# Two Strassen pairs in the output projection, their weight sums on GpSimd, and a new order around them

## The chip, the cores and the metric

One Trainium2 chip, one core of it. Every array is float32. The metric is the time of one execution of the whole program on the device, in microseconds (us); for the kernel before it is the median of three executions. The engines are TensorE (PE), VectorE (DVE), ScalarE (ACT), GpSimd (POOL) and SyncE (SP, which only issues transfers here).

## The reference, cut to what matters

One inference step of a two-layer streaming encoder, for a prompt of 256 frames and a running stream of 64 (T = 320 columns in all), at a width of 1024:

```python
for l in range(DEPTH):                      # 2 layers
    h = rms(x, norm_mix) ; proj = h @ w_in  # 14 pieces of different mixers
    y_a = head_rms(RG-LRU(conv(lru_x))) * gelu(lru_g)      # recurrence
    y_b = head_rms(latent attention)
    y_c = head_rms(retention(rope(r_q), rope(r_k), r_v)) * silu(r_g)
    y_d = head_rms(mLSTM) * sigmoid(m_o)
    x = x + concat([y_a, y_b, y_c, y_d]) @ w_out           # the output projection: 1024 x 1024
    x = x + SwiGLU(rms(x, norm_ffn))                       # hidden width 2816
```

It also returns the new states of each mixer. The line with `w_out` is what the change touches.

## The kernel before, in words

Activations lie transposed: a tile is 128 features by 320 columns, so x is 8 tiles (`xT`), the mixers' output 8 tiles (`mixT`: 0 and 1 the recurrence's, 2 and 3 attention's, 4 and 5 retention's, 6 and 7 mLSTM's). Weights come in chunks of 1 MB through a ring of five slots: SP loads chunk g once the last use of chunk g - 5 has ended (`LAST_USE`, lines 200 to 204). The four chunks of `w_out` are o0 to o3; each holds two output units of 128 features for all 8 input tiles. They are followed by f0, f1 and so on of the feed-forward part.

Every engine's program is written out by hand, in order, and engines meet at semaphores. `need` and `wait_filled` wait, `step` signals and also waits for the instruction's own end. PSUM has eight banks; `layer_uses` lists every use of a bank in a layer, `claim` lets PE wait until the use before it in the same bank has been read (`now_read`). The first head mean, `cm0`, follows the retention scores `cs2` in bank 2, which DVE reads in `weights_c(2)`.

**Strassen pairs.** Most products of the kernel are already done in a form with seven half-size products in place of eight. Two output units and 320 columns are split into 2 x 2 blocks (pairs of input tiles, halves of 160 columns). POOL makes three sums of the weight blocks by four instructions of 128x512 (`pair_weights`, lines 638 to 664, for chunks of `w_in`; `mix_weights`, 666 to 683, for the feed-forward part), the last of which signals `mixed`. Four sums of activations are made by DVE or POOL. PE runs seven products of four matmuls of 160 columns each into three banks a, b and c, and DVE adds them up in the pattern of lines 1978 to 1988 or 2406 to 2426, after ACT has copied the first product (`p1_copied`).

**The output projection** (`project(n, ks)`, line 1287) is not in this form: unit n takes one matmul of 320 columns for each of the 8 input tiles, 64 in all. The order is by what is ready: tiles 6, 7 (mLSTM) and 2, 3 (attention) first, between retention's last steps; then the recurrence's statistics `am0`, `am1` (line 1317) when `h_sq` is there; then tiles 0, 1 and 4, 5. DVE adds each finished unit to x (line 2333), ACT squares it and applies the gain (`squares`, lines 1523 and 1525), DVE sums the squares (line 2337), and PE sums them over the features (`ms2`, line 1352) in the middle of the 16 plain matmuls of the first feed-forward unit (`first_units`, line 1356).

**Around it, on the other engines.** POOL rotates retention's queries and keys (`rotate`, lines 750 to 766), stores retention's states as `c_pair` makes them, stores the recurrence's inputs and states and signals `a_out`; in layer 0 it then reloads the latents and their weights for layer 1 (`load_latents`), and goes on to the feed-forward weight sums. DVE, after the pair `rg` (1978 to 1988) and its clamp (2250), makes the recurrence's exponents (2254), retention's weights (`weights_c`, lines 2111 and 2275, four times), the recurrence's arguments (2284 to 2290), retention's gate (2293), attention's last tile (2205), `c_pair` (2264 to 2268), and the scans (2315, 2316). ACT does the roots and exponentials between. At the end DVE makes `mix0` (2325, 2326; tiles 0 and 1) and then `mix2` (2329; tiles 4 and 5).

Of the kernel before, what the change touches and what calls it, by code (L numbers as in the profile page):

```python
# [16 lines left out]
ALU = mybir.AluOpType  # L17
# [46 lines left out]
NPAIR = len(PAIRS)  # L64
MIXES = FT - 1 + 3 * NQ
MADE = NPAIR + MIXES
P1S = NPAIR + FT - 1 + NQ
# [62 lines left out]
def layer_uses():  # L130
# [44 lines left out]
    u += [(f"o{n}", (n,)) for n in range(KT)]  # L175
# [26 lines left out]
LAST_USE.update({f"o{i}": f"o{2 * i + 1}" for i in range(4)})  # L202
# [4 lines left out]
def build(nc, I, O):  # L207
    with ExitStack() as ctx:
# [136 lines left out]
        xgm = mixT  # L345
        hp = mixT[:, :, :].rearrange("p k n -> p (k n)").rearrange("p (s k n) -> p s k n", s=4, k=4)
# [273 lines left out]
        def _(pool):  # L620
# [44 lines left out]

            def mix_weights(l, i):
# [37 lines left out]
            for l in range(DEPTH):  # L704
# [63 lines left out]
                for grp in "dc":  # L768
                    if grp == "c":
# [45 lines left out]
        def _(pe):  # L815
# [240 lines left out]
            for l in range(DEPTH):  # L1056
# [230 lines left out]
                def project(n, ks):  # L1287
# [5 lines left out]
                    for k in ks:  # L1293
                        need(pe, f"mix{k // 2}", l, 1)
                        ins = mm(bank(u, 0, T), w[:, k, (n % 2) * P:(n % 2 + 1) * P], mixT[:, k, :],  # L1295
                                 start=(k == 6), stop=(k == 5), skip_group_check=True)
                    if ks[-1] == 5:
                        fill(ins, u)
# [14 lines left out]
                project(4, (6, 7, 2, 3))  # L1313
# [4 lines left out]
                project(5, (6, 7, 2, 3))  # L1318
                for n in range(2):
                    project(n, (0, 1))  # L1320
                for n in range(2):
                    project(n, (4, 5))
                for n in range(2, 6):
                    project(n, (0, 1, 4, 5))
                for n in range(6, KT):
                    project(n, (6, 7, 2, 3, 0, 1, 4, 5))

                def product(use, l, i, p, right, opens, closes):
# [3 lines left out]
                    if p in (3, 5, 6, 7):  # L1332
                        need(pe, "mixed", l, MADE, NPAIR + i + 1)
# [156 lines left out]
        def _(act):  # L1490
# [49 lines left out]
            for l in range(DEPTH):  # L1540
# [250 lines left out]
                squares(l, 1)  # L1791
# [43 lines left out]
        def _(dve):  # L1835
# [96 lines left out]
            for l in range(DEPTH):  # L1932
# [395 lines left out]
                need(dve, "c_rstd", l, 2)  # L2328
                step(v.tensor_tensor(mixT[:, 4:6, :], ycm[:, :, :], ysm[:, :, :], ALU.mult), "mix2")

                for n in range(KT):
# [3 lines left out]
                    if n > 1:  # L2335
                        need(dve, "squared", l, 2 * KT, KT + n)
# [136 lines left out]
```

How the kernel before makes its waits and increments, by code:

```python
        def wait_filled(eng, use, l):  # L420
            k = banks[use][0]
            eng.wait_ge(filled[k], l * nfill[k] + order[use])
# [1 line left out]
        def claim(pe, use, l):  # L425
            for prev in before[use]:
                if prev is not None:
                    k = banks[prev][0]
                    pe.wait_ge(read[k], l * nfill[k] + order[prev])
                elif l > 0:
                    for k in {banks[last[b_]][0] for b_ in banks[use]}:
                        pe.wait_ge(read[k], l * nfill[k])
                else:
                    top = max(banks[use])
                    pe.wait_ge(sem("x_turned"), top + 1)
                    if 0 in banks[use]:
                        pe.wait_ge(sem("cols_ready"), 1)
# [8 lines left out]
        def need(eng, name, l, n, k=None):  # L447
            assert per.setdefault(name, n) == n, name
            eng.wait_ge(sem(name), l * n + (n if k is None else k))
# [3 lines left out]
            def step(ins, name=None, bank_read=None):  # L454
                if bank_read is not None:
                    use, l = bank_read
                    k = banks[use][0]
                    ins.then_inc(read[k], 1)
                    eng.wait_ge(read[k], l * nfill[k] + order[use])
                    return
                k = name or chain
                made[k] = made.get(k, 0) + 1
                ins.then_inc(sem(k), 1)
                eng.wait_ge(sem(k), made[k])
# [11 lines left out]
        def wait_bank_read(eng, use, l):  # L476
            k = banks[use][0]
            eng.wait_ge(read[k], l * nfill[k] + order[use])
```

## Time and profile before

| | |
|---|---|
| median of 3 executions | 906.52 us (906.29 to 907.2) |
| profiled execution | 906.72 us, of which the span is 904.9 us |
| PE busy | 894.6 us (99% of the span) |
| POOL busy | 512.4 us (57%) |
| DVE busy | 511.4 us (57%) |
| ACT busy | 226.7 us (25%) |
| granted TensorE clock | 1.0 |
| moved by DMA | 112.92 MB, a mean of 125 GB/s |

The span runs from the first to the last instruction of the profile; times in the rows below count from its start. A row of the timeline has start, duration, engine, line, operation and shape, and in brackets how long the engine stood idle before and for whom. Layer 0 takes the first half of the span, layer 1 the second; the feed-forward part is more than half of each.

### The profile page before, as it was taken

Reading aid. Unit: us, or ns where it says so; the run is one execution under the profiler, and the core shown is the slowest. Engines: PE = TensorE matmul, PEld = TensorE weight load, DVE = VectorE, ACT = ScalarE, POOL = GpSimd, SP = SyncE. Lnnn points to the kernel's source line nnn. Section 1 sums busy time; section 2 is a strip of 40 time slices with the busy share of each in tenths; the row PEclk is TensorE's granted clock in tenths of the full one; section 3 lists DMA queues with packets and bytes.
Section 4 is the critical chain, followed back from the end, with each engine's and each line's share of the span. In section 5 each row is a group of like instructions: output and inputs, shape, how many; then the busy total and the mean of one; then the engine's idle time right before and its main releaser. Section 6 shows DMA issues by size and latency. Waiting matters only on the chain.

```text
span 904.9 us, 15545 instructions
## 1 busy us (share of the span) xinstructions
PE 894.6 (99%) x5984; PEld 812.3 (90%) x5984; DVE 511.4 (57%) x1001; ACT 226.7 (25%) x497; POOL 512.4 (57%) x514
## 2 busy tenths in 40 slices
PE   8999999999999999999999999999999999999998
PEld 6897878668999999999979878776799999999998
DVE  6677857735656565522366776575465656563221
ACT  3334356632000000100133334574300000000001
POOL 6861574316966666676457345902287666666770
PEclk9999999999999999999999999999999999999999
DMA  9979331239444444433444773121855545434421
GB/s 274 233 152 106 108 93 49 53 65 256 140 138 139 139 137 137 129 128 129 125 131 144 34 152 96 48 90 14 183 140 140 141 140 140 141 129 128 147 88 36
DMA packets 159091, 112.92 MB, mean 125 GB/s; under 512 B 9829, under 2 KB 156682, under 8 KB 158890
## 3 DMA queue, kind: packets, MB, share of 16 engines
q1 hardware_dynamic: 154402, 104.44, 40.2%
q0 software_dynamic: 3984, 6.74, 7.3%
q8 instruction: 48, 0.79, 0.4%
q10 hardware_dynamic: 632, 0.75, 0.3%
q14 instruction: 25, 0.20, 0.1%
HBM read 108.33 MB, written 2.27 MB: 122 GB/s over the span
## 4 chain that ended last, share of the span: by engine, by line
PE 90%; ACT 4%; DVE 4%; DMA 1%; issue 1%; POOL 0%; SPq 0%; DVEq 0%; ACTq 0%; POOLq 0%
PE ps L1338 53%; PE ps L1295 7%; PE ps L905 7%; PE ps L871 6%; PE ps L891 2%; PE ps L1356 2%; PE ps L1093 2%; PE ps L1062 1%; PE ps L1125 1%; PE ps L1221 1%; DMA arena<-in_x_sample 1%; PE ps L1229 1%; PE ps L1005 1%; DVE work L2119 1%; DVE arena L2222 0%
## 5 line engine op out<-in xcount | busy, mean ns | idle before, releaser
L680 POOL TENSOR_TENSOR work<-ring 128x512 f32<-128x512 f32 (+1 forms) x66 | 81.9, 1240 | 155.6 <-issue 111.0
L1338 PE MATMUL ps<-mixT,ring 128*128 128x160 f32 x672 | 105.0, 299 | 0.0
L1338 PE MATMUL ps<-hT,work 128*128 128x160 f32 x672 | 98.5, 299 | 0.0
L1338 PE MATMUL ps<-hT,ring 128*128 128x160 f32 x672 | 98.1, 299 | 0.0
L1338 PEld LDWEIGHTS ps<-mixT,ring 128*128 128x128 f32 x672 | 95.8, 190 | 0.0
L1338 PEld LDWEIGHTS ps<-hT,ring 128*128 128x128 f32 x672 | 93.7, 190 | 0.3
L1338 PEld LDWEIGHTS ps<-hT,work 128*128 128x128 f32 x672 | 93.7, 190 | 0.0
L681 POOL TENSOR_TENSOR ring<-ring 128x512 f32<-128x512 f32 (+1 forms) x66 | 82.6, 1252 | 5.2
L682 POOL TENSOR_TENSOR work<-ring 128x512 f32<-128x512 f32 (+1 forms) x66 | 82.0, 1243 | 5.2
L683 POOL TENSOR_TENSOR work<-ring,work 128x512 f32<-128x512 f32 (+1 forms) x66 | 81.9, 1240 | 5.2
L1805 ACT ACTIVATE arena<-ps 128x160 f32<-128x160 f32 x42 | 12.8, 304 | 286.8 <-PE ps L1338 286.8
L871 PE MATMUL ps<-hT,ring 128*128 128x320 f32 x256 | 72.9, 436 | 0.0
L1295 PE MATMUL ps<-mixT,ring 128*128 128x320 f32 x256 | 70.9, 434 | 0.9 <-DVE mixT L2326 0.9
L2406 DVE TENSOR_TENSOR arena<-arena,ps 128x160 f32<-128x160 f32 x8 | 2.6, 321 | 118.6 <-ACT arena L1823 118.6
L1295 PEld LDWEIGHTS ps<-mixT,ring 128*128 128x128 f32 x256 | 48.3, 190 | 21.6 <-issue 1.8
L871 PEld LDWEIGHTS ps<-hT,ring 128*128 128x128 f32 x256 | 47.4, 190 | 18.9 <-issue 1.0
L1338 PE MATMUL ps<-work,ring 128*128 128x160 f32 x352 | 55.6, 299 | 0.0
L1338 PE MATMUL ps<-mixT,work 128*128 128x160 f32 x336 | 52.5, 299 | 0.0
L1338 PE MATMUL ps<-arena,work 128*128 128x160 f32 x352 | 51.7, 299 | 0.0
L1338 PEld LDWEIGHTS ps<-work,ring 128*128 128x128 f32 x352 | 50.4, 190 | 0.0
L1338 PEld LDWEIGHTS ps<-arena,work 128*128 128x128 f32 x352 | 49.1, 190 | 0.0
L1338 PE MATMUL ps<-arena,ring 128*128 128x160 f32 x330 | 48.7, 299 | 0.0
(455 smaller groups left out, 1623.9 us busy)
## 6 DMA issues: line engine op xcount, KB each, us to landing
ring<-in_w_gu SPq DMA_DIRECT2D x88, 512.0 KB, 5.2
ring<-in_w_in SPq DMA_DIRECT2D x44, 512.0 KB, 6.7
ring<-in_w_down SPq DMA_DIRECT2D x32, 512.0 KB, 4.5
ring<-in_w_out SPq DMA_DIRECT2D x16, 512.0 KB, 4.9
ring<-in_w_down SPq DMA_DIRECT2D x16, 384.0 KB, 3.6
cst<-in_consts POOLq DMA_DIRECT2D x1, 1664.0 KB, 12.8
ring<-in_w_in SPq DMA_DIRECT2D x2, 640.0 KB, 5.7
arena<-r POOLq DMA_DIRECT2D x8, 160.0 KB, 18.0
```

The costliest lines, as they stand in the source:

```text
L680: step(tt(s3, a11, a21, ALU.subtract))
L681: step(tt(a21, a21, a22, ALU.add))
L682: step(tt(s2, a21, a11, ALU.subtract))
L683: step(tt(s4, a12, s2, ALU.subtract), "mixed")
L871: ins = mm(bank(use, 0, T, m), w[:, k, c:c + m], right[:, k, 0:T], start=(k == 0), stop=(k == KT - 1))
L891: ins = mm(bank(use, at * HT, HT), left, right, start=(opens and k == 0), stop=(k == KT // 2 - 1), skip_group_check=True)
L905: ins = mm(bank(use, at * HT, HT), left(k), right(k), start=(opens and k == 0), stop=(k == KT // 2 - 1), skip_group_check=True)
L1093: ins = mm(bank("kvr", t * 168, 168), hT[:, k, t * P:(t + 1) * P], w[:, k, :], start=(k == 0), stop=(k == KT - 1))
L1295: ins = mm(bank(u, 0, T), w[:, k, (n % 2) * P:(n % 2 + 1) * P], mixT[:, k, :], start=(k == 6), stop=(k == 5), skip_group_check=True)
L1338: ins = mm(bank(use, at * HT, HT), left, right(k), start=(opens and k == 0 and at == 0), stop=(closes and k == n - 1), skip_group_check=True)
L1356: return mm(bank(use, 0, T), w[:, k, q * P:(q + 1) * P], xg[:, k, :], start=(k == 0), stop=(k == KT - 1))
L1805: step(A(p1c[:, j % 2, :], bank(f"fa{j}", 0, HT), ACT.Copy), "p1_copied")
```

## The change

Units 4 to 7 (chunks o2 and o3) become two Strassen pairs, p2 and p3; units 0 to 3 stay as they were. POOL makes their weight sums right after the fourth rotation, behind a wait for `bo1` (the last reading of the attention probabilities, whose room the sums take). PE has a new order; ACT squares the recurrence's state before retention's second root; DVE makes `mix2` before `mix0`, then four sums of `mixT`, and adds up two pairs. In layer 0 `load_latents` waits for the end of both pairs, for the sums also lie in the latents' room. The counters `MADE` and `P1S` grow by two.

```diff
@@ layer_uses @@
-    u += [(f"o{n}", (n,)) for n in range(KT)]
+    u += [(f"o{n}", (n,)) for n in range(4)]
+    u += [("p2a", (4,)), ("p2c", (5,)), ("p3a", (6,)), ("p3c", (7,)), ("p2b", (0,)), ("p3b", (1,))]
@@ LAST_USE @@
-LAST_USE.update({f"o{i}": f"o{2 * i + 1}" for i in range(4)})
+LAST_USE.update({f"o{i}": f"p{i}c" if i in OUTS else f"o{2 * i + 1}" for i in range(4)})
@@ POOL @@
+            def out_weights(l, i):
+                name = f"o{OUTS[i]}"
+                w, _ = quarters(name, l)
+                s2, s3, s4 = osum[i]
+                if i == 0:
+                    wait_filled(pool, "bo1", l)
                 wait_chunk(pool, name, l)
                 a11, a12, a21, a22 = w[:, :, 0, 0, :], w[:, :, 1, 0, :], w[:, :, 0, 1, :], w[:, :, 1, 1, :]
                 tt = nc.gpsimd.tensor_tensor
...
                         for n in range(4):
                             rotate(n)
+                        for i in range(len(OUTS)):
+                            out_weights(l, i)
...
-                    wait_filled(pool, "kv2", l)
+                    for p in OUTS:
+                        wait_filled(pool, f"p{p}c", l)
                     load_latents(l + 1)
@@ PE @@
-                project(4, (6, 7, 2, 3))
+                early, late, every = (3, 1), (2,), (3, 1, 2, 0)
+                out_product(2, 1, early, opens=True)
+                out_product(2, 2, early)
+                out_product(2, 3, early, opens=True)
                 need(pe, "h_sq", l, 1)
...
-                project(5, (6, 7, 2, 3))
-                for n in range(2):
+                for n in range(4):
+                    project(n, (4, 5))
+                for which in (1, 2, 3):
+                    out_product(2, which, late)
+                out_product(3, 1, early + late, opens=True)
+                out_product(3, 2, early + late)
+                for n in range(4):
                     project(n, (0, 1))
-                for n in range(2):
-                    project(n, (4, 5))
-                for n in range(2, 6):
-                    project(n, (0, 1, 4, 5))
-                for n in range(6, KT):
-                    project(n, (6, 7, 2, 3, 0, 1, 4, 5))
+                for which in (1, 2, 3):
+                    out_product(2, which, (0,))
+                for which in (1, 2):
+                    out_product(3, which, (0,))
+                out_product(2, 6, every, closes=True)
+                out_product(2, 5, every, opens=True)
+                out_product(2, 7, every, closes=True)
+                out_product(2, 4, every, closes=True)
+                out_product(3, 6, every, closes=True)
+                out_product(3, 5, every, opens=True)
+                out_product(3, 7, every, closes=True)
+                out_product(3, 3, every, opens=True)
+                out_product(3, 4, every, closes=True)
@@ ACT @@
-                pair_rstd(1)
                 need(act, "lru_scanned", l, 1)
                 step(A(fl(an), fl(ah), ACT.Square), "h_sq")
+                pair_rstd(1)
...
-                squares(l, 1)
+                squares(l, 1, range(4))
+                for p in OUTS:
+                    need(act, "x_new", l, 2 * KT, 2 * p)
+                    wait_filled(act, f"p{p}a", l)
+                    step(A(pair_p1, bank(f"p{p}a", 0, HT), ACT.Copy), "p1_copied")
+                    squares(l, 1, range(2 * p, 2 * p + 2))
@@ DVE @@
+                need(dve, "c_rstd", l, 2)
+                step(v.tensor_tensor(mixT[:, 4:6, :], ycm[:, :, :], ysm[:, :, :], ALU.mult), "mix2")
                 for k in range(2):
                     need(dve, "a_rstd", l, 2, k + 1)
...
-                need(dve, "c_rstd", l, 2)
-                step(v.tensor_tensor(mixT[:, 4:6, :], ycm[:, :, :], ysm[:, :, :], ALU.mult), "mix2")
-
-                for n in range(KT):
+                m_at = lambda j, t: mixT[:, j::2, t * HT:(t + 1) * HT]
+                step(v.tensor_tensor(msum[0], m_at(0, 1), m_at(0, 0), ALU.subtract), "mix_sums")
+                step(v.tensor_tensor(msum[2], m_at(1, 1), msum[0], ALU.subtract), "mix_sums")
+                step(v.tensor_tensor(msum[1], m_at(1, 1), m_at(0, 1), ALU.subtract), "mix_sums")
+                step(v.tensor_tensor(msum[3], m_at(1, 0), msum[2], ALU.subtract), "mix_sums")
...
+                def out_pair(p):
+                    a, b_, c = (f"p{p}{x}" for x in "abc")
...
+                    need(dve, "p1_copied", l, P1S, NPAIR + OUTS.index(p) + 1)
+                    step(v.tensor_tensor(pair_u2, pair_p1, bank(a, HT, HT), ALU.add))
+                    step(v.tensor_tensor(x11, x11, pair_p1, ALU.add))
+                    step(v.tensor_tensor(x11, x11, bank(a, 2 * HT, HT), ALU.add), bank_read=(a, l))
+                    wait_filled(dve, b_, l)
...
+                    step(v.tensor_tensor(x22, x22, pair_u34[:, HT:T], ALU.add))
+                    step(v.tensor_tensor(x22, x22, bank(b_, 0, HT), ALU.add), bank_read=(b_, l))
+                    step(v.tensor_tensor(mid, mid, pair_u34, ALU.add))
+                    wait_filled(dve, c, l)
+                    step(v.tensor_tensor(mid, mid, bank(c, 0, T), ALU.add), "x_new")
+                    now_read(dve, c)
+                    now_made(dve, "x_new")
+
+                for n in range(4):
                     wait_filled(dve, f"o{n}", l)
...
+                for p in OUTS:
+                    squares_so_far(2 * p)
+                    out_pair(p)
+                    squares_so_far(2 * p + 1)
```

`out_product(p, which, ks)` runs product `which` of pair p for the tile pairs ks, one matmul of 160 columns for each; products 3, 5, 6 and 7 wait for `mixed`, products 4 to 7 for all four `mix_sums`. Tile pair k is made of `mixT` tiles 2k and 2k + 1. The four weight-sum instructions of `out_weights` are those of `pair_weights`.

## Rows read from the trace of the kernel before

**Rows 1.** The page, part 1: busy time, share of the span and instructions of each engine.

```profile
PE 894.6 (99%) x5984; PEld 812.3 (90%) x5984; DVE 511.4 (57%) x1001; ACT 226.7 (25%) x497; POOL 512.4 (57%) x514
```

**Rows 2.** The timeline, PE and its weight loads, layer 0: start us, us, instruction [idle before].

```profile
149.86 0.22 PE L1005 MATMUL ps<-work,arena 128*64 128x64 f32 x1
...
157.49 0.99 PE L1005 MATMUL ps<-work 128*64 128x256 f32 x12
...
164.58 0.30 PEld L1036 LDWEIGHTS ps<-work,cst 128*128 128x128 f32 x2 [0.62 <-DVEq L469]
...
175.96 2.32 PE L1295 MATMUL ps<-mixT,ring 128*128 128x320 f32 x8
```

**Rows 3.** The chain of waits: start us, us, what. Layer 0, from the output projection on.

```profile
182.02 21.77 PE ps L1295 x80
...
206.48 1.08 PE ps L1352 x4
...
213.48 237.71 PE ps L1338 x1750
```

**Rows 4.** DVE and POOL out of SBUF at once; the last is L2214's min/median/max ns.

```profile
47.38 1.32 DVE L1986 TENSOR_SCALAR work<-work 128x640 f32<-128x640 f32 x1
...
229.68 1.27 POOL L682 TENSOR_TENSOR work<-ring 128x512 f32<-128x512 f32 x1
...
231.03 1.27 POOL L683 TENSOR_TENSOR work<-ring,work 128x512 f32<-128x512 f32 x1
...
231.17 1.32 DVE L2389 TENSOR_TENSOR arena<-arena 128x160 f32<-128x160 f32 x1
...
L2214 DVE TENSOR_SCALAR wqb<-arena,cols x4: 447/449/542, 128.7 to 579.5; 128x323 f32<-128x323 f32 x4
```

**Rows 5.** The timeline, POOL, from the key rotation's end to the feed-forward sums, layer 0.

```profile
163.16 0.61 POOL L691 DMA_DIRECT2D out_p_ret<-sst  x1 [16.82 <-DVE sst L2265]
...
198.30 0.76 POOL L698 DMA_DIRECT2D pckv<-in_cache_mla_ckv  x1 [17.00 <-DMA out_s_lru_h<-arena]
...
203.67 1.26 POOL L680 TENSOR_TENSOR work<-ring 128x512 f32<-128x512 f32 x1 [3.33 <-DMA ring<-in_w_gu]
```

**Rows 6.** The w_out loads: SyncE's issues in the timeline, and on the page their landing.

```profile
131.58 18.06 SPq L587 DMA_DIRECT2D ring<-in_w_out  x4
...
ring<-in_w_out SPq DMA_DIRECT2D x16, 512.0 KB, 4.9
```

**Rows 7.** The timeline, DVE adds that read PSUM in the down projection, POOL at work.

```profile
391.32 0.32 DVE L2406 TENSOR_TENSOR arena<-arena,ps 128x160 f32<-128x160 f32 x1 [13.19 <-ACT arena L1823]
...
393.11 0.49 DVE L2414 TENSOR_TENSOR arena<-ps,arena 128x320 f32<-128x320 f32 x1
```

**Rows 8.** The timeline, DVE, from the end of rg's pair to the recurrence's result, layer 0.

```profile
150.62 0.49 DVE L2250 TENSOR_SCALAR work<-work 128x640 f32<-128x640 f32 x1
...
152.46 0.81 DVE L2254 TENSOR_SCALAR arena<-arena,c 128x323 f32<-128x323 f32 x2 [1.34 <-ACT arena L1513]
...
153.70 0.82 DVE L2275 TENSOR_TENSOR work<-ps,cst 128x384 f32<-128x384 f32 x2
...
156.56 0.83 DVE L2285 TENSOR_TENSOR arena<-arena,wqb 128x646 f32<-128x646 f32 x1
...
157.42 0.50 DVE L2287 TENSOR_SCALAR arena<-arena 128x646 f32<-128x646 f32 x1
...
159.02 1.14 DVE L2293 SCALAR_TENSOR_TENSOR work<-work,cols 128x320 f32<-128x320 f32 x2
...
161.29 0.55 DVE L2205 SCALAR_TENSOR_TENSOR mixT<-ps,cols,arena 128x320 f32<-128x320 f32 x1 [1.13 <-ACT arena L1731]
...
176.78 1.14 DVE L2321 SCALAR_TENSOR_TENSOR arena<-arena,cols 128x323 f32<-128x323 f32 x2
```

**Rows 9.** The timeline, ACT: square and gain of one x tile behind the projection, layer 0.

```profile
204.48 0.47 ACT L1523 ACTIVATE hT<-xT 128x320 f32<-128x320 f32 x1 [3.24 <-DVE xT L2333]
...
204.98 0.56 ACT L1525 ACTIVATE work<-xT,cols 128x320 f32<-128x320 f32 x1
```

More of the change, by code:

```diff
@@ L64 @@
 NPAIR = len(PAIRS)
+OUTS = (2, 3)
 MIXES = FT - 1 + 3 * NQ
-MADE = NPAIR + MIXES
-P1S = NPAIR + FT - 1 + NQ
+MADE = NPAIR + len(OUTS) + MIXES
+P1S = NPAIR + len(OUTS) + FT - 1 + NQ
 MSLOTS = 3
@@ L345, in build @@
         xgm = mixT
+        low = MSLOTS * 3 * 512 + KT * T
+        msum = [x.rearrange("p (k n) -> p k n", n=HT) for x in
+                (work[:, low:low + 4 * HT], work[:, low + 4 * HT:low + 8 * HT], work[:, low + 8 * HT:low + 12 * HT],
+                 arena[:, 2 * 326:2 * 326 + 4 * HT])]
+        pT1 = ytm_at + 640
+        osum = [[x.rearrange("p (k n) -> p k n", n=P) for x in three] for three in
+                ((pT0[:, 0:512], pT0[:, 512:1024], wkvb[:, :]),
+                 (work[:, pT1:pT1 + 512], work[:, pT1 + 512:pT1 + 1024], pckv[:, :, :].rearrange("p a n -> p (a n)")))]
         hp = mixT[:, :, :].rearrange("p k n -> p (k n)").rearrange("p (s k n) -> p s k n", s=4, k=4)
@@ L664, in pair_weights @@
                 step(tt(s4, a12, s2, ALU.subtract), "mixed")
+            def out_weights(l, i):
[4 more added lines that the diff above has]
+                    wait_filled(pool, "bo1", l)
+                wait_chunk(pool, name, l)
+                a11, a12, a21, a22 = w[:, :, 0, 0, :], w[:, :, 1, 0, :], w[:, :, 0, 1, :], w[:, :, 1, 1, :]
+                tt = nc.gpsimd.tensor_tensor
+                step(tt(s3, a11, a21, ALU.subtract))
+                step(tt(a21, a21, a22, ALU.add))
+                step(tt(s2, a21, a11, ALU.subtract))
+                step(tt(s4, a12, s2, ALU.subtract), "mixed")
             def mix_weights(l, i):
@@ L1312, in _, with out_product @@
                 pair_mean(1, l)
-                project(4, (6, 7, 2, 3))
+                def out_product(p, which, ks, opens=False, closes=False):
+                    i = OUTS.index(p)
+                    use = f"p{p}" + {1: "a", 2: "a", 6: "a", 5: "b", 7: "b", 3: "c", 4: "c"}[which]
+                    if opens:
+                        claim(pe, use, l)
+                    wait_chunk(pe, f"o{p}", l)
+                    if which in (3, 5, 6, 7):
+                        need(pe, "mixed", l, MADE, NPAIR + i + 1)
+                    if which in (4, 5, 6, 7):
+                        need(pe, "mix_sums", l, 4)
+                    w, _ = quarters(f"o{p}", l)
+                    at = {1: 0, 2: 2, 6: 1, 5: 0, 7: 1, 3: 0, 4: 1}[which]
+                    for k in ks:
+                        need(pe, f"mix{k}", l, 1)
+                        left = {1: w[:, k, 0, 0, :], 2: w[:, k, 1, 0, :], 3: osum[i][2][:, k, :],
+                                4: w[:, k, 1, 1, :], 5: w[:, k, 0, 1, :], 6: osum[i][0][:, k, :],
+                                7: osum[i][1][:, k, :]}[which]
+                        right = {1: mixT[:, 2 * k, 0:HT], 2: mixT[:, 2 * k + 1, 0:HT], 3: mixT[:, 2 * k + 1, HT:T],
+                                 4: msum[3][:, k, :], 5: msum[0][:, k, :], 6: msum[2][:, k, :], 7: msum[1][:, k, :]}[which]
+                        ins = mm(bank(use, at * HT, HT), left, right, start=(opens and k == ks[0]), stop=(k == 0),
+                                 skip_group_check=True)
+                    if closes:
+                        fill(ins, use)
+                early, late, every = (3, 1), (2,), (3, 1, 2, 0)
+                out_product(2, 1, early, opens=True)
+                out_product(2, 2, early)
+                out_product(2, 3, early, opens=True)
                 need(pe, "h_sq", l, 1)
@@ L1332, in product @@
                     if p in (3, 5, 6, 7):
-                        need(pe, "mixed", l, MADE, NPAIR + i + 1)
+                        need(pe, "mixed", l, MADE, NPAIR + len(OUTS) + i + 1)
                     for k in range(n):
```

21 lines of the change are left out of this document (14 added, 7 removed).

## The prediction

> **What bounds the kernel.** I read the page's busy shares first: TensorE (PE) is busy 99% of the span [rows 1], so time goes only where PE loses instructions or is made to wait. The chain of waits then shows the layer's one weak stretch: it leaves PE for ScalarE (ACT) and VectorE (DVE) in the middle of the mixers, comes back to PE with the first head mean at 164.6 [rows 2], and leaves it once more for the recurrence's statistics, before the output projection's last 80 records at 182.0 [rows 3]. From there on PE runs without a gap. Layer 1 repeats the pieces of layer 0 one for one, so all steps below are counted in layer 0 and doubled.
>
> Prices of PE: a matmul call leaves two records. 80 records of 320 columns took 21.77 us, so a call costs 0.544; 1750 records of 160 columns took 237.71, so a half call costs 0.272 [rows 3]. Halving the columns halves the price exactly.
>
> **PE work.** Units 4 to 7 lose 4 x 8 = 32 calls, 17.4 us. Two Strassen pairs add 2 x 7 x 4 = 56 half calls, 15.2 us. That is -2.2 us a layer, if nothing waits.
>
> **GpSimd's (POOL) eight weight sums.** POOL waits for `bo1`, the last matmul of which ends at 150.1 [rows 2], so the sums start at about 150.15. One costs 1.27, and the next begins 1.35 after it, a gap of 0.08 [rows 4]: four take 5.4, eight 10.8, some 0.7 more where DVE stretches them. They end at 161.4 to 161.7. POOL stood idle for 16.8 us until the state's store at 163.2 [rows 5], so the stores queued behind (retention's state, the recurrence's, `a_out`) start on time by themselves. Chunk o3 can only load once `rgc` is filled: its load is issued by 149.6 and takes about 4.9 [rows 6], so it lands at 154.5, before the second four sums (155.7). Nothing waits for weights: PE first wants a sum after 176.
>
> **What the sums do to DVE is the heart of it.** Rows of the feed-forward stage show what happens when both engines work out of SBUF: a DVE sum of 160 columns out of SBUF took 1.32; it began while POOL's sum of 231.03 to 232.30 ran and ended 0.19 after it [rows 4]. An add of the same size that reads PSUM took 0.32, and one of 320 columns 0.49, with POOL at work too [rows 7]. A clamp of 640 columns, 0.49 when POOL is idle [rows 8], took 1.32 in POOL's company [rows 4]. So a DVE instruction of this kind waits for POOL's running instruction and then does its own work (0.19 for 160 columns; for the fast 640 I take 0.35, between that and its whole 0.49). Those that read PSUM keep their price. From 150.6 to 160.2 DVE has twelve instructions out of SBUF [rows 8] (one row stands for a repeated kind; the two L2111 have 192 columns).
>
> I lay them against POOL's sums (end of sum n: 151.4, 152.9, 154.25, 155.6, 156.95, 158.3, 159.75, 161.4). Clamp L2250: ends 151.8. The two L2254 (input there at 152.46): 153.1 and 154.4. Tail weights L2111: 155.8; two PSUM multiplies, 156.7; L2111: 157.15; two more multiplies, 158.05. L2284: 158.65. L2285: 160.4. L2287: 161.75. Then POOL is done, and L2288, L2290 and two L2293 take 2.25: 164.0, against 160.2 before. DVE is 3.85 late. It used to wait 1.13 before L2205 [rows 8], which absorbs that much, so L2205 begins at 164.05 instead of 161.29: **2.75 us late**.
>
> Is L2254 (323 columns, one SBUF input) really blocked? Two took 0.81, so 0.41 each, against 0.50 for twice the columns [rows 8], the rate of the blocked clamp; yet its like, L2214, ran between 0.45 and 0.54 beside POOL [rows 4], hardly touched. If it is free, the schedule above ends 0.3 earlier (2.45). I take blocked, for the rate is what it shares with the clamp; both ends stay in the range. The Trainium skill ("SBUF — State Buffer", Who interferes with whom) says that a DVE instruction with two SBUF inputs, or in a two-port mode, and a GpSimd one lock each other out for a whole instruction, and that one with a single SBUF input outside those modes is free: by the first half the lateness is 2.75, by the second, if L2254 falls there, 2.45.
>
> Who is queued behind: L2205, c_pair(0), then weights_c(2), whose end frees the bank that PE claims for the first head mean. PE's weight load there sat 0.62 waiting for DVE [rows 2], so the step has no slack: PE, and everything behind it, goes 2.75 late as well. Earlier, weights_c(1) ends at 158.05 instead of 155.9, and pair_out(0), at 157.5 before [rows 2], waits 0.6; this lies inside the 2.75. I call the lateness d. Bounds from the rows: each sum could block a little less where DVE arrives late in it (d = 1.6), or stretch POOL more (3.4).
>
> **From the head mean to the norm's sum.** Before: the head mean at 164.58 [rows 2], the projection's end E = 182.02 + 21.77 = 203.79, ms2 filled at 206.48 + 1.08 = 207.56 [rows 3].  After, times without d: the second head mean ends at 176.1, where the four calls of unit 4 began before [rows 2]; six half calls, 177.75; by then `h_sq` stands, since ACT does it right after the scan, ahead of a reciprocal root (about 1.0 by two passes); two statistics matmuls, 178.85. mix2 now comes first: DVE is free at 177.9, after L2321 [rows 8], 0.82 more, so PE starts (4,5) at 178.95; 8 calls, 183.3; 9 half calls, 185.75; (0,1) with 8 calls, 190.1; 5 half calls, 191.45; 36 half calls, E = 201.25. ACT reaches the recurrence's roots some 0.4 earlier than before, so mix0 is ready at 181.5, and the four `mix_sums` (0.83 each, with a gap 0.86, by L2285 [rows 8]) at 185: they hide behind the 4.35 and 2.45 of PE work before (0,1), and would cost only if they came 6 us later. Removed waits and work together: 2.5.
>
> The tail loses some back. Before, only tile 7 was open at E; now tiles 6 and 7 are finished by one add, and ACT's queue makes it late: p2's last add ends at E - 4.15; two squares and two gains (0.47, 0.56 each [rows 9]), E - 1.95; copy of p3's first product (0.3, an estimate from 0.47 for twice the columns), E - 1.6; DVE's three adds, E - 0.5; then 0.49, 0.32, 0.32 [rows 7]: bank p3b is read at E + 0.75. PE claims that bank ahead of the norm's units, so it waits 0.83. The last adds end at E + 1.8, tile 7's square at E + 3.4, in time for the norm matmuls. ms2 is filled at E + 4.6 = 205.85 + d against 207.56: **d - 1.7** a layer.
>
> One collision more. POOL's first feed-forward sum began at 203.67, released by its chunk's DMA [rows 5], which trickles until the recurrence's small stores land at 198.3 [rows 5]. With stores d late it begins at 206.4, E + 2.4 or so. There DVE adds square 6 into the sum (0.49); caught behind the sum, it ends at E + 4.05 and PE waits 0.5. Even odds: +0.25 a layer. The latents' reload, now behind p3c, is issued by E + 2 and is needed only in layer 1.
>
> **Sum.** 2 x (2.75 - 1.7 + 0.25) = +2.6. The profiled execution took 906.72 (span 904.9), 0.2 above the median of 906.52; the sum is a difference and goes onto the median: 909.1. A measurement of this kernel can tell about 0.2% (1.8 us) from no change: faster is under 904.7, slower over 908.3.
>
> **Rivals.**
> 1. *DVE's wait is partly absorbed* (d = 1 to 2: DVE comes late into each sum, L2254 is free, ACT's order gives slack). Speaks for it: half the schedule hangs on tenths of a microsecond. Against: eight DVE instructions meet eight sums, and what DVE has left when POOL ends is over 2 us. At d = 1.7 the two effects cancel and the collision alone is left: 906.5 to 907, within 0.2%. Chance 0.26.
> 2. *Other side: DVE gets through the sums.* If DVE's instruction, once issued, goes ahead and POOL waits, DVE is delayed by almost nothing (whoever is first goes first). The place is L2254 to L2287, and it decides at d under 0.8. Then 2 x -1.7 = -3.4: 903.1. Against it: on DVE's side POOL came first [rows 4], and its gaps of 0.08 in 1.35 leave DVE hardly a turn. Chance 0.17. The Trainium skill (same page and section) states that issue order, not the kind of operation, decides who blocks.
> 3. *Half calls don't save*: if a half call cost over 0.311 (17.4 / 56), the pairs save nothing, and each layer ends at d - 1.7 + 2.2, about 913 in all. The 1750 records speak against it. Chance 0.03, on the slow side.
>
> **Numbers.** The forecast itself (d 2.2 to 3.4) gives 907.5 to 910.9, with and without the collision; chance 0.54. With rival 3, slower is 0.57; same 0.26; faster 0.17. The range reaches down to the upper part of the faster case, leaving about 0.12 of it out, and up past the forecast's own end by half a microsecond, leaving out most of rival 3: 904.0 to 911.4.
>
> **What would show it.** DVE's L2111, L2284, L2285 and L2287 near 155 to 162 at 0.7 to 1.4 each, each ending 0.2 to 0.7 after a POOL sum; POOL idle no longer before 161; PE's wait for DVE at the first head mean 2 to 3 us, twice; head mean to ms2 41.3 us instead of 43.0; a wait for DVE's read before the norm units; DVE idle before L2205 gone. Wrong if the head mean starts under 1 us late, if those DVE instructions keep 0.36 to 0.83, or if PE waits for mix_sums or a `mixed`.

## The result and the profile after

The changed kernel took **919.5 us** (median of four runs, 917.9 to 920.4) against 906.4 us for the kernel before on the same chip: ratio 1.0145, 95% interval 1.0129 to 1.0162. Slower, as forecast, but by 13 us and not by 2.6; the time lies outside the range of 904.0 to 911.4. The profiled execution took 917.87 us, span 916.1.

The page, part 1, of the changed kernel (against [rows 1]):

```profile
PE 896.9 (98%) x6080; PEld 822.1 (90%) x6080; DVE 536.3 (59%) x1033; ACT 227.9 (25%) x501; POOL 535.1 (58%) x530
```

PE has 96 records more (in each layer 56 half calls for 32 calls, two records each), and DVE is busy 25 us longer for 32 instructions more. The first place is where the prediction put it. GpSimd's sums and VectorE beside them, timeline of layer 0 (start us, us, instruction, [idle before]; PE's last step ahead of this stretch, L1249, starts 0.57 earlier than in the kernel before, 134.21 against 134.78):

```profile
152.49 1.28 POOL L688 TENSOR_TENSOR arena<-ring 128x512 f32<-128x512 f32 x1
153.85 1.28 POOL L689 TENSOR_TENSOR wkvb<-ring,arena 128x512 f32<-128x512 f32 x1
...
159.41 1.56 POOL L689 TENSOR_TENSOR pckv<-ring,work 128x512 f32<-128x512 f32 x1
```

```profile
153.99 1.35 DVE L2183 TENSOR_TENSOR work<-work,cst 128x192 f32<-128x192 f32 x1
155.38 0.82 DVE L2347 TENSOR_TENSOR work<-ps,cst 128x384 f32<-128x384 f32 x2
...
157.70 0.50 DVE L2356 TENSOR_SCALAR arena<-arena 128x646 f32<-128x646 f32 x1
158.23 1.78 DVE L2357 TENSOR_TENSOR arena<-arena,wqb 128x646 f32<-128x646 f32 x1
160.05 1.27 DVE L2359 TENSOR_SCALAR arena<-arena 128x646 f32<-128x646 f32 x1
...
163.59 0.55 DVE L2277 SCALAR_TENSOR_TENSOR mixT<-ps,cols,arena 128x320 f32<-128x320 f32 x1
```

A tail weight (192 columns) took 1.35, against 0.36 for its like at 156.34, and the 646-column product 1.78 against 0.83 [rows 8], each ending 0.2 to 0.7 after a POOL sum; the multiplies that read PSUM kept 0.41 each. L2277, L2205 of before, has no idle time ahead of it any more.

The chain of waits of the changed kernel, layer 0, from the first head mean to the feed-forward (against [rows 2, 3]; start us, us, what):

```profile
166.89 0.81 PE ps L1064 x2
167.70 4.92 PE ps L1323 x12
172.62 1.38 PE ps L1033 x28
174.00 5.58 PE ps L1323 x20
...
193.90 11.14 PE ps L1360 x82
205.03 2.48 issue
207.52 4.36 PE ps L1423 x10
211.88 1.34 PE ps L1419 x4
213.22 5.92 PE ps L1423 x22
```

Three things are to be read here. The head mean is 2.3 later, 2.9 with the earlier start. Twelve records then take 4.92 (layer 1 has 4.79), where 80 of the same kind at the full clock take 21.77 [rows 3], so 3.27 for twelve. And PE stands still 2.48 ahead of the norm's units (2.34 in layer 1), where I had 0.83, and the ten records behind that take 4.36 (4.62). The granted clock in windows of 2 us shows why (stretch, PE busy, PEclk, DMA share, GB/s; 1.00 is 2.4 GHz, 0.50 is 1.2 GHz):

```profile
168.00:170.00 2.00, 2.00 (x5) 0.50 1.00 276
170.00:172.00 2.00, 2.00 (x7) 0.67 0.00 0
208.00:210.00 2.00, 2.00 (x7) 0.72 1.09 305
210.00:212.00 2.00, 2.00 (x5) 0.50 1.05 325
```

The clock fell to its lower level just after each of the two waits. The norm's sum (`ms2`) is filled at 213.22 against 207.56 [rows 3]: with the earlier start, 6.2 us in this layer; counted in the same way, layer 1 loses 5.5.

Why PE waited at the projection's end: VectorE (timeline, layer 0) and ScalarE (layer 1) stand still in the middle of p2's adds, though what they read is ready.

```profile
197.59 0.32 DVE L2420 TENSOR_TENSOR xT<-xT,ps 128x160 f32<-128x160 f32 x1
200.09 0.49 DVE L2422 TENSOR_TENSOR pair_t<-ps,pair_t 128x320 f32<-128x320 f32 x1 [2.18 <-PE ps L1360]
...
207.35 1.99 DVE L2427 TENSOR_TENSOR xT<-xT,pair_t 128x320 f32<-128x320 f32 x1
...
646.01 0.30 ACT L1862 ACTIVATE pair_t<-ps 128x160 f32<-128x160 f32 x1 [2.69 <-remote]
```

The products that DVE adds at 200.09 had ended by 198.5, and the one that ACT copies at 646.01 by 644.0 (PE's timeline), so up to 1.6 and 2.0 us of the idle time are not PE's doing. The row at 207.35 is another matter: p3's add of 0.49 ran into POOL's first feed-forward sum. "Remote" is the profile's word for a releaser that it doesn't know. The windows over all engines of the same stretch (PE, PEld, DVE, ACT, POOL, then clock, DMA share, GB/s) gave the clue:

```profile
194.00:196.00 2.00, 2.00 (x17) 2.00 (x16) 1.47 (x3) 1.61 (x4) 0.00 (x0) 1.00 0.18 31
196.00:198.00 2.00, 2.00 (x17) 2.00 (x16) 0.97 (x3) 0.30 (x1) 0.00 (x0) 1.00 0.19 32
198.00:200.00 2.00, 2.00 (x17) 2.00 (x17) 0.00 (x0) 0.00 (x0) 0.00 (x0) 1.00 0.30 24
```

The feed-forward's weight load, whose issue began at 191.78, moves 24 to 32 GB/s from 194 to 200 and 284 to 331 from 204 on. The four stores of the recurrence's last state (`_lru_h`, 512 B each, one element per partition) were issued from 181.48 to 183.64; in the kernel before they were issued by 181.31 and had landed at 198.30 [rows 5]. Loads and engines seemed to come free when stores of that kind land. That was a coincidence of times until the runs below, and the kernel before shows that it can't be the whole story. The same windows of its trace:

```profile
194.00:196.00 2.00, 2.00 (x9) 1.45 (x8) 0.82 (x3) 0.88 (x3) 0.00 (x0) 1.00 0.47 28
196.00:198.00 2.00, 2.00 (x9) 1.37 (x9) 0.41 (x1) 0.90 (x2) 0.00 (x0) 1.00 0.83 57
```

There the load trickled too, but DVE and ACT did their adds and squares all the while.

### The profile page after: what moved, and what is told of

It is laid out like the page before. It is cut to its first block, busy times and chain, and to the rows that moved or that the text cites. A ratio compares the mean times of both kernels' runs of the same rounds, so it can differ in the third digit from the quotient of the medians.

```text
span 916.1 us, 15858 instructions
## 1 busy us (share of the span) xinstructions
PE 896.9 (98%) x6080; PEld 822.1 (90%) x6080; DVE 536.3 (59%) x1033; ACT 227.9 (25%) x501; POOL 535.1 (58%) x530
## 4 chain that ended last, share of the span: by engine, by line
PE 83%; DVE 10%; ACT 2%; issue 2%; DMA 1%; POOL 0%; SPq 0%; DVEq 0%; ACTq 0%; POOLq 0%
PE ps L1405 53%; PE ps L899 6%; PE ps L1323 4%; PE ps L933 3%; PE ps L1360 3%; PE ps L919 2%; PE ps L1423 2%; PE ps L1249 1%; PE ps L1121 1%; DMA arena<-in_x_sample 1%; PE ps L1090 1%; DVE work L2191 1%; PE ps L1257 1%; PE ps L1033 1%; DVE work L2183 1%
## 5 line engine op out<-in xcount | busy, mean ns | idle before, releaser
L1405 PEld LDWEIGHTS ps<-mixT,ring 128*128 128x128 f32 x672 | 95.8, 190 | 0.0
L2510 DVE TENSOR_TENSOR arena<-arena,ps 128x160 f32<-128x160 f32 x8 | 2.6, 322 | 118.6 <-ACT arena L1895 118.6
L1405 PEld LDWEIGHTS ps<-mixT,work 128*128 128x128 f32 x336 | 47.9, 190 | 0.0
L2472 DVE TENSOR_TENSOR arena<-arena,ps 128x160 f32<-128x160 f32 x42 | 13.5, 321 | 56.2 <-ACT arena L1877 55.5
```

The lines of the kernel that those rows point to most:

```text
L1405: ins = mm(bank(use, at * HT, HT), left, right(k), start=(opens and k == 0 and at == 0), stop=(closes and k == n - 1), skip_group_check=True)
L2472: step(v.tensor_tensor(u2, p1, bank(fa, HT, HT), ALU.add))
```

## The experiments

Where a stall or a wait is given without a fence, it is the timeline's or the chain's row of that run. "L0" and "L1" are the layers. Each ratio is to the kernel before on the same chip; its median there was 905.7 to 906.4, so a difference between medians of two groups of runs can be off by 0.7 us. Line numbers shift by a few between kernels: the projection is L1323 to L1328, the pairs' products L1360 to L1365, the norm's units L1423 to L1428.

### The weight sums, each way

**e1_no_sums.** GpSimd makes no sums; products 3, 6 and 7 of p2 and p3 take plain weight blocks, so that units 4 to 7 are not the reference's.

```
 def out_weights(l, i):
     ...
-    step(tt(s3, a11, a21, ALU.subtract))
-    step(tt(a21, a21, a22, ALU.add))
-    step(tt(s2, a21, a11, ALU.subtract))
-    step(tt(s4, a12, s2, ALU.subtract), "mixed")
+    now_made(pool, "mixed")
```

> The changed kernel without its eight weight sums on GpSimd; the products that would use them take unsummed weight blocks of the same size (so units 4 to 7 are not the reference's). Theory (the sums keep VectorE from SBUF, TensorE waits at the first head mean and comes back at half clock): the wait of 2.3 us and the 1.7 us at half clock vanish in both layers, and the whole lateness with them: 2 x (2.9 + 1.7) = 9.2 us less, about 910.3; the wait of 2.4 us before the norm units stays. Rival (the lateness at the head mean is absorbed by slack later, and all the loss sits behind the projection): 917 to 919.5.

Measured: 914.0 us, ratio to the kernel before 1.0089 (1.0073 to 1.0104), between the theory and its rival. The head mean's wait and the slow records behind it are gone, the tail is worse: DVE stands 3.43 in L0, ACT 4.11 in L1, both "remote", and PE waits 4.7 and 4.4. Of 13 us the sums explain 5.5, and the rest is elsewhere.

**e2_before_sums.** The kernel before, with eight sums of this size on GpSimd behind the rotations, into a tile nobody reads.

```
 for n in range(4):
     rotate(n)
+wait_filled(pool, "bo1", l)
+dc = C("decay").rearrange("p (s n) -> p s n", s=4)
+for _ in range(8):
+    step(nc.gpsimd.tensor_tensor(pT0[:, 0:512], dc[:, 0, :], dc[:, 1, :], ALU.subtract))
```

> The kernel before, with eight GpSimd instructions of the same size (128x512, two SBUF inputs) at the same place, whose result nobody uses. Theory (lock plus clock): the head mean 2.7 to 3 us late, then 1.7 us at half clock, twice: 914 to 916, with VectorE's SBUF instructions stretched as in the changed kernel. Without the clock's part: 912. Rival (only the new order of the projection makes the loss): 906.4.

Measured: 915.2 us, ratio 1.0098 (1.0083 to 1.0113), as the theory had it. The head mean starts at 167.45 in L0. Sums alone, with no pair at all, cost the old kernel 8.8 us; the pairs do not have to be there. In the profiled execution, whose span is 7.7 longer than before, the twelve records behind the wait took 3.23 in L0 and 4.92 in L1, after waits of 2.4 both times. So lateness is about 6 of this and the clock the rest (the four runs had a mean granted clock of 0.996 to 0.998).

### The tail and the head mean's wait, with the stores in place

**e3_tail.** ACT copies p3's first product ahead of squares 4 and 5, DVE adds p3 ahead of those squares.

```
-    squares(l, 1, range(2 * p, 2 * p + 2))
+    if p == 3:
+        squares(l, 1, range(4, 6))
+squares(l, 1, range(6, 8))
...
-for p in OUTS:
-    squares_so_far(2 * p)
-    out_pair(p)
-    squares_so_far(2 * p + 1)
+squares_so_far(4)
+out_pair(2)
+out_pair(3)
+for n in (5, 6, 7):
+    squares_so_far(n)
```

> The changed kernel, with ScalarE copying p3's first product before it squares x tiles 4 and 5, and VectorE adding p3 before it adds those squares. Theory (TensorE waits 2.4 us for the read of bank p3b because of this queue, and the wait halves its clock for 1.7 to 1.9 us): p3b is read before the projection ends, so 2 x (2.4 + 1.8) = 8.4 us less, about 911. If the clock would have fallen anyway: 914.7. Rival (the adds are late for another reason, GpSimd's lock or code fetch): over 916.

Measured: 917.1 us, 1.0106 (1.0081 to 1.0131), the rival's side; the gain of 2.4 lies within overlapping intervals. The reason is in this row of ACT's timeline; the copy's input stood ready from 194.8 on:

```profile
200.83 0.30 ACT L1862 ACTIVATE pair_t<-ps 128x160 f32<-128x160 f32 x1 [6.70 <-remote]
```

**e4_fill.** PE makes units 0 and 1 of chunks 6 and 7 ahead of the head mean.

```
+for n in range(2):
+    project(n, (6, 7))
 pair_mean(0, l)
-for n in range(3):
+for n in range(2, 3):
     project(n, (6, 7))
```

> The changed kernel with four calls of the projection (units 0 and 1, tiles 6 and 7, 2.2 us) moved ahead of the first head mean, into TensorE's wait. Theory: the wait shrinks to 0.1 to 0.3 us and the clock stays full there (3.4 us less for both layers); TensorE's lead of 2.2 us is mostly lost again at h_sq and mix2, which follow VectorE: 914 to 917. If a short wait halves the clock as well: 919. If the lead is kept: 911 to 912.

Measured: 921.0 us, 1.0168 (1.0145 to 1.0191), slower than any of the cases expected. The wait at the head mean is gone and nothing is won: DVE now stands 5.38 "remote" in L0 and resumes at 202.11, ACT 3.60 in L1. In every variant the stall ends some 15 to 18 us after the last of the four stores is issued: 183.64 to 200.09 and 631.25 to 646.01 (the changed kernel), 180.7 to 197.05 (e1), 184.9 to 200.83 (e3), 183.96 to 202.11 (e4).

### The stores

**e8_no_last_stores** leaves the four stores out of each layer (those outputs stay unwritten). **e9_late_stores** moves them, in the changed kernel, behind the second chunk's feed-forward sums; **e10_before_late_stores** does that to the kernel before.

```
 need(pool, "lru_scanned", l, 1)
-for s, (pre, e) in enumerate((("p", SEQ - 1), ("s", AW - 1))):
-    for k in range(2):
-        out(O[pre + "_lru_h"][l, :, k * P:(k + 1) * P].rearrange("b p -> p b"), ah[:, k, e:e + 1])
+for m, e in enumerate((SEQ - 1, AW - 1)):
+    step(nc.gpsimd.tensor_copy(hl[:, l, m, :], ah[:, :, e]))
...
 for i in range(MIXES):
     mix_weights(l, i)
+    if i == 1:
+        for m, pre in enumerate(("p", "s")):
+            for k in range(2):
+                out(O[pre + "_lru_h"][l, :, k * P:(k + 1) * P].rearrange("b p -> p b"),
+                    hl[:, l, m, k:k + 1])
```

> The changed kernel without the four stores of the recurrence's last state (each 512 B, one element per partition; their outputs stay unwritten). Theory A, these stores hold back what DVE or ACT stand for behind the releaser 'remote' until about 16 us after the stores' issue (resumed at 200.09 and 646.01): with the stores gone DVE starts p2's adds at about 198.5 (when its second product is filled), PE's wait ahead of p3's third product falls from 2.5 and 2.3 us to about 0.8, and the clock does not fall there: 919.5 less 2 x (1.6 + 1.7) = about 913, certainly under 915.5. Theory B, the stores are a bystander: 918 to 921, with the stalls of after still there.

Measured: 913.9 us, 1.0091 (1.0074 to 1.0108), as theory A had it. DVE's row at 197.30 has 1.07 ahead of it, all of it PE's.

> The changed kernel with the same four stores moved behind the weight sums of the feed-forward's second chunk (their eight numbers first copied by GpSimd to a tile of their own, two copies of under 0.3 us). Theory A: as without the stores, 912 to 916, unless the stall only moves to where new instructions are needed some 16 us after the new issue, which would show as a 'remote' wait in the feed-forward and leave 917 to 920. Theory B: 918 to 921.

Measured: **911.4 us**, 1.0063 (1.0041 to 1.0085), 8.1 us off the changed kernel (7.4 by the two ratios). No row of the two stretches has "remote" any more. Windows and chain of this run, as above:

```profile
194.00:196.00 2.00, 2.00 (x17) 2.00 (x16) 0.81 (x3) 0.70 (x2) 0.00 (x0) 1.00 1.18 311
196.00:198.00 2.00, 2.00 (x17) 2.00 (x17) 0.90 (x3) 0.00 (x0) 0.00 (x0) 1.00 1.20 291
```

```profile
166.94 0.81 PE ps L1068 x2
167.75 3.23 PE ps L1327 x12
...
192.59 11.14 PE ps L1364 x82
203.72 1.36 issue
205.09 2.93 PE ps L1427 x10
208.02 0.04 issue
208.06 1.34 PE ps L1423 x4
```

The load runs at 311 GB/s where it trickled, PE waits 1.36 (1.61 in L1) instead of 2.48, and the clock holds in both places of L0; in L1 the head mean's twelve records still took 4.92. Of its four runs two had a mean granted clock of 1.0 (910.2 and 910.4 us) and two less (912.4 and 913.7).

> The kernel before with the same move of the stores. Both theories: no or little gain, 905 to 907, since its tail shows no such stall; a gain of over 2 us would mean that the kernel before paid for the stores too, and then the comparison with the moved stores in both is what the change costs by itself.

Measured: 906.0 us, 1.0001 (0.9991 to 1.0010). Its chain of waits, for the comparison with e9's (same start of the layer):

```profile
164.09 0.81 PE ps L1040 x2
...
203.29 2.69 PE ps L1360 x10
205.99 1.08 PE ps L1356 x4
```

The kernel before did not pay for these stores; the changed one does. That the change put work which DVE and ACT owe PE at once into the time in which such a stall can fall is my reading; why no instruction of the kernel before was held, though both engines worked all that time, no run shows.

**e18_half_stores** leaves two of the four where they were and moves two.

> The changed kernel with two of the four stores of the recurrence's last state at their old place and two moved. If the stall lasts as long as the elements left in the queue take, it is over some 6 to 8 us sooner than with four: DVE or ACT resume before 195 us of layer 0, where nothing is yet ready, and the time is that of the run with all moved, 911 to 913. If any such store holds the engines until about 16 us after its issue: 915 to 919.

Measured: 920.6 us, 1.0174 (1.0158 to 1.0191), the second expectation's side and even over its bound. ACT's row in L1 reads

```profile
645.90 0.30 ACT L1868 ACTIVATE pair_t<-ps 128x160 f32<-128x160 f32 x1 [3.11 <-remote]
```

and the load again trickles until 200 in L0. The stall does not grow with the number of elements: two such stores are as bad as four.

### Which part of the rest is whose

**e14_no_sums_late_stores** is e1's edit on top of e9 (units 4 to 7 again not the reference's).

> The changed kernel with the stores moved and its eight weight sums left out (products 3, 6 and 7 take blocks as loaded, so units 4 to 7 are not the reference's). It prices the sums where no store stall is mixed in: 911.4 less 2 x 2.85 and some clock = 904 to 905.5. If it stays above 907, the sums are not what the rest of the loss is made of.

Measured: 905.9 us, 0.9999 (0.9990 to 1.0008). The head mean is at 164.01, against 166.94 in e9 and 164.09 in e10. With neither sums nor stall, and with the tail as the change has it, the change is worth nothing either way. Together with e1 this gives each part twice: the sums 5.5 us with the stores in place (e1) and 5.5 with the stores moved (this run), the stores 8.1 with the sums (e9) and 8.1 without (e1 against this run), where no record behind the head mean is slow in either.

**e11_late_stores_tail** is e3's edit on top of e9. **e19_tail_late_stores** keeps the running squares apart: 4 ahead of p3's second product, 5 ahead of its last.

```
 def out_pair(p):
     ...
+    if p == 3:
+        squares_so_far(4)
     wait_filled(dve, b_, l)
     ...
+    if p == 3:
+        squares_so_far(5)
     wait_filled(dve, c, l)
```

> The changed kernel with the stores moved and, in the tail, ScalarE's copy of p3's first product ahead of squares 4 and 5 and DVE's adds of p3 ahead of those running sums. Theory A: the reordering lost in the earlier run only because ScalarE stood still 6.7 us ahead of that copy; now that is gone and the reordering takes another 0.5 to 1 us per layer off: 910 to 914. Theory B: as in the earlier run, about 917.

> The changed kernel with the stores moved and the tail reordered (first product of p3 copied ahead of squares 4 and 5, those two running sums between p3's adds), the weight sums where the change has them. Expected 1 to 2 us under the run with late stores alone (911.4): 909.5 to 910.5. Rival: no gain, 911 to 912, as the last two running sums decide.

Measured: 910.9 (1.0041 to 1.0071) and 910.2 us (1.0036 to 1.0063) against 911.4, both inside what was expected. A gain of about a microsecond is not shown, for the intervals overlap e9's.

**e15_fill_late_stores** is e4's edit on top of e9.

> The changed kernel with the stores moved and PE's wait at the head mean filled with units 0 and 1 of the projection (chunks 6 and 7), which stood behind it. The head mean itself then comes up to 1 us later, the 2.3 us wait is gone, the clock has no reason to fall there, and the rest is 2.2 us earlier if nothing else waits for the head mean: 911.4 less 2 x 1.5 to 2.3 = 907 to 908.5. Rival: the head mean's other readers (retention's mix) become late and take it back: 910 to 912.

Measured: 913.4 us, 1.0079 (1.0064 to 1.0095): the rival's side and past its bound. The wait of 2.3 became waits of 0.8 for the mixes, 0.6 and 0.3 for ACT, and the tail's wait in L1 rose to 2.7. Here a wait that was due to a late input was only moved by reordering the waiter.

### Where the sums can go

**e12_late_sums_stores** is e9 with the sums behind the recurrence's copies, and p2's third product made late. **e13_both_late_tail** adds e19's tail.

```
     step(nc.gpsimd.tensor_copy(hl[:, l, m, :], ah[:, :, e]))
+for i in range(len(OUTS)):
+    out_weights(l, i)
...
+out_product(2, 3, every, opens=True)
 out_product(2, 4, every, closes=True)
```

> The changed kernel with the recurrence's last stores moved as before and its eight weight sums moved too: GpSimd makes them behind the copies of the recurrence's last state, from about 179 to 190 us of layer 0, where it stood idle until 204, and p2's third product is made after the others. If the head mean's lateness (2.85 us per layer, 166.94 against 164.09) came from the sums alone, the head mean is back at about 163.6 and both clock falls behind it are gone: 911.4 less 2 x 2.85 less some 1 = about 904.5 (903 to 906). Rival: the sums now slow the mixes (182 to 187) and the running squares, and PE waits there instead: 907 to 910.

> The same with the tail reordered: ScalarE copies p3's first product before it squares units 4 and 5, and DVE adds those two squares between p3's adds instead of ahead of them. Expected: the wait ahead of the feed-forward's third product falls from 1.4 and 1.6 us to about 0.8, 903.5 (902 to 905.5), so a little faster than the kernel before (905.8). Rival: the running sums of 6 and 7 come later under GpSimd's lock and take the gain back: 904 to 907.

Measured: 911.8 us, 1.0059 (1.0045 to 1.0073), and 909.3 us, 1.0033 (1.0022 to 1.0043). Both missed their forecast: the same loss in another place. DVE's timeline of e12:

```profile
183.81 1.80 DVE L2408 TENSOR_TENSOR work<-mixT,work 128x640 f32<-128x640 f32 x1
185.65 1.77 DVE L2409 TENSOR_TENSOR work<-mixT 128x640 f32<-128x640 f32 x1
187.46 1.77 DVE L2410 TENSOR_TENSOR arena<-mixT,work 128x640 f32<-128x640 f32 x1
```

The sums of the mixes, 0.82 each in e9, now took 1.8 to 1.9, and four of POOL's eight sums were drawn out to 1.75 as well: the two engines took turns.

**e16_sums_behind_mix** is e13 with one wait more, **e17_sums_behind_mix_only** is e12 with it.

```
+need(pool, "mix_sums", l, 4)
 for i in range(len(OUTS)):
     out_weights(l, i)
```

> The changed kernel with the stores moved, the tail reordered as in the last run but one of its kind, and GpSimd's eight weight sums begun only when VectorE has made the mixes' sums (about 184 us of layer 0), so that they run to about 196 beside the residual adds that read PSUM. If it was the pairing of SBUF operations that cost 5.5 us wherever it stood, the mixes are back at 0.82 us, the products find their sums in time, and the time is 903 to 905, under the kernel before (905.9). Rival: the sums stretch the running squares and p2's adds as much and the tail starts late: 906 to 909.

> The same without the reordered tail. Expected 1 to 2 us over it: 905 to 906.5, that is, the time of the run in which the sums were left out (905.9). Rival: 908 or more, if the sums cost something beside the tail's adds.

Measured: **903.8 us, ratio 0.9975 (0.9965 to 0.9984)** and 905.9 us, 1.0004 (0.9995 to 1.0013). Both as expected; e16 is the one run here that is faster than the kernel before, by 0.25%. POOL's timeline and the chain of waits of e16, L0:

```profile
183.89 1.27 POOL L687 TENSOR_TENSOR arena<-ring 128x512 f32<-128x512 f32 x1 [4.50 <-DVE arena L2413]
...
193.66 1.09 POOL L690 TENSOR_TENSOR pckv<-ring,work 128x512 f32<-128x512 f32 x1
```

```profile
189.52 11.95 PE ps L1365 x88
201.48 2.69 PE ps L1428 x10
204.17 1.09 PE ps L1424 x4
```

The sums now lie beside residual adds that read PSUM; one add out of SBUF took 1.18 and one running square 0.81 (0.49 elsewhere), nothing else was hit. In L0 PE goes from the projection into the norm's units without a wait (0.79 in L1), and the norm's sum is filled at 205.26.

## Why the prediction was right and wrong, point by point

(E is the projection's end, d the lateness of the head mean, as in the prediction.)

- **PE's work** (-2.2 a layer): right. Half calls cost half: 82 records in 11.14 is 0.272 a call.
- **d = 2.75, by POOL's sums delaying DVE**: right in place, mechanism and size: 2.9 in the changed kernel; 166.94 - 164.09 = 2.85 between e9 and e10. L2254 (now L2326), which I doubted, took 2.06 for two instead of 0.81 [rows 8]: it is blocked, while its like L2214 ran beside POOL almost untouched [rows 4]; what sets the two apart stays open. The Trainium skill ("SBUF — State Buffer", Who interferes with whom) lists such an operation, `tensor_scalar`, among those that can enter a two-port mode and then contend with GpSimd; the 2.06 us agree with the contention, and the mode itself is in no row.
- **Head mean to E, -2.5**: 203.29 - 164.09 = 39.20 in e10 and 203.72 - 166.94 = 36.78 in e9, so -2.4. mix2, h_sq and mix_sums hid as stated.
- **The tail, net +0.8 there, +0.25 for a collision**: the working was right in kind and short by a half where nothing disturbs it: PE waits 1.36 and 1.61 in e9 for the 0.83 forecast. DVE's three adds began at E - 1.1 and ended at E - 0.1, not E - 0.5, behind a copy at E - 1.5, and gaps of 0.04 between adds were left out. The ten records behind took 0.24 and the four statistics 0.26 more than e10's. Together e9's norm sum is filled 2.34 later than e10's in L0, where the sum of my terms with d = 2.85 was 2.85 - 1.7 + 0.25 = 1.4. Twice that difference is 1.9 us. e14 shows it without the sums: from the head mean to the norm's sum 42.5 in L0 and 43.4 in L1 (a wait of 2.6), against 43.0 in both layers of e10, so that nothing was gained where I had 2 x 1.45.
- **The step that failed**: "ACT's queue makes it late: p2's last add ends at E - 4.15". It took DVE and ACT as free to work behind the recurrence's stores. In L0 p2's last add ended at 202.34, E - 2.7, since DVE stood until 200.09, 16.5 us after the last of these stores was issued; in L1 it was ACT that stood, until 646.01. With the stores moved it ended at 199.92, E - 3.8 (e9). I had used the stores' landing at 198.3 [rows 5] to say when POOL's feed-forward sum begins, and did not ask what else may wait so long. The stores in place cost 919.5 - 911.4 = 8.1 us (e9), and 0 in the kernel before (e10).
- **Where the 8.1 lie** is only in part to be seen, for the two profiled executions differ by 5.5 (917.87 and 912.39). In L0 the norm's sum is filled 213.22 - 209.40 = 3.8 later than in e9: 1.7 of slow records behind the head mean, 1.1 of longer wait, 1.4 of slow records behind that wait, less 0.4 elsewhere. The first 1.7 are not the stores': the head mean starts at 166.89, and they are issued from 181.48 on. That leaves 2.1 for them in L0 and 2.4 in L1 (0.7 of wait, 1.7 of slow records behind it). The pair of runs without the sums, where nothing is slow behind the head mean, has all of it in the tail: from the head mean to the norm's sum e1 took 4.5 us longer than e14 in L0 and 3.5 in L1.
- **What no step held**: the clock. At 1.2 GHz twelve records take 4.9 and not 3.2, ten 4.4 to 4.6 and not 2.9. The changed kernel's profile has four such places, e9's one, e16's none. I had priced a wait of PE at its length alone and put the clock at nothing, without a reason.
- **Rivals.** Rival 1 (partly absorbed) and rival 2 (DVE gets through) are refuted by the timeline, rival 3 by the half calls.
- **The whole**: +13.1 = 5.5 by the sums (e9 less e14) + 8.1 by the stores + (-0.5) left, most of which is the difference between the chips: by the ratios the sum is 5.8 + 7.4 - 0.1. For everything else nothing is left, as e14 against the kernel before shows. My +2.6 was 2 x 2.75 for the sums, against 2 x (-1.7 + 0.25) for the rest, where the rest is worth nothing. So the forecast that the change is slower came true, but 8.1 of the 10.4 us beyond it come with the stores, which had no term in it.

## What to carry to other kernels

A change that takes work off the busiest engine is worth what its helpers leave of it: 2.2 us of PE a layer were gone, and 2.85 came back through eight GpSimd sums placed beside VectorE's SBUF work on the critical path, but nothing when the same sums lay beside adds out of PSUM (e17 against e14, 905.9 both). Before adding work that one engine owes another at once, look what is in flight at that time: element-wise stores that cost nothing in the old order cost 8 us in the new one. Moving them was worth about as much as all the reordering of the engines together (7.6 us, from 911.4 in e9 to 903.8 in e16). Price a wait of TensorE above about 2 us with the chance that the clock falls, here 1.4 to 1.7 us each time.

## What the hardware showed that I had not expected

- **Element-wise stores hold others up.** After two or four stores of 128 single elements each, a load moved 23 to 33 GB/s instead of about 300 for some 6 us (the changed kernel and e18, 194 to 200), and DVE or ACT stood still though what they read was ready, until 15 to 18 us after the issue. The stores' own packets were over by 186. That the stores are the cause is shown (e8 and e9 against the changed kernel, and e18 against e9, which has the same copies). It is not that nothing gets through: DVE and ACT ran ten or more instructions each behind the stores, in the changed kernel before they stopped and in the kernel before without a stop. The stores of 1.5 KB that go ahead of them (`_lru_conv`) stayed in place in e9 and held nothing. How the stores stop an engine is open: the packets of the two instruction queues came at 204 to 206 in the changed kernel and at 198 to 200 in e9, which would fit instructions that arrive late, but DVE resumed at 200.09, ahead of them, and no run here separates this. The Trainium skill ("DMA: Bandwidth & Descriptors", Specifications) says that a transfer below 512 B makes the DMA engine read, modify and write; a store here is 512 B in all, in pieces of 4 B, and no run shows whether this is what takes so long. In e9 the moved stores made a load trickle at 3 to 57 GB/s from 228 to 236, in the feed-forward, where no engine stood still.
- **The same wait, two clocks.** A wait of 2.3 to 2.4 us at the head mean stands in both layers of eight profiles (the changed kernel, e2, e3, e8, e9, e11, e18, e19). In seven of these sixteen places the records behind it ran at the full clock (both layers of e3 and e8, L0 of e2 and e9, L1 of e11), in nine the twelve took 4.2 to 4.9. At the tail, waits of 1.4 to 1.6 (e8, e9, e14, e15, e17) cost no clock; 2.6 in e14's L1 cost none either, but 2.2 in e8's L1 and 2.3 in the changed kernel's L1 did. What decides it stays open.
- **Stores left out were not faster than stores moved** (913.9 against 911.4, intervals just overlapping at 1.0074 to 1.0085). The clock can account for it: e8's four runs had a mean granted clock of 0.994 to 0.998, two of e9's had 1.0, and the two profiled executions, both at 0.998, took 912.47 and 912.39. In e8's L1 a feed-forward sum of POOL met p2's add (1.15 for 0.49) and PE waited 2.2 instead of 1.6.
